# Differential attention: the weighted values from f16 high and low pieces, two banks for the transposes, the extreme kept scaled and negated

## The chip, the core and the metric

The kernel runs on one core of a Trainium2 chip. The metric is device time in microseconds of one execution; lower is better. TensorE (PE) multiplies and transposes, VectorE (DVE) and ScalarE (ACT) work on what it leaves in PSUM, GpSimd (POOL) takes a few element-wise steps, and SyncE (SP) issues most transfers. Each engine works through its own queue in order and waits on semaphores for the others.

## The reference, cut to what matters

One layer of a hybrid encoder: RMSNorm, one projection, four mixers (gated linear attention, a gated recurrence, differential attention, gated DeltaNet), a gated merge, cross attention over memory tokens, and a mixture of experts. The change touches differential attention alone. SEQ is 1024, there are 4 heads, two maps m of width 32 per head, and values 64 wide:

```python
        bias = -slopes[:, None, None] * dist
        s = jnp.einsum('bhmqd,bhmkd->bhmqk', q_blk, kt) + bias[None, :, None]
        p = jax.nn.softmax(s, axis=-1)
        attn = p[:, :, 0] - lam * p[:, :, 1]
        return jnp.einsum('bhqk,bhkd->bhqd', attn, vt)
```

After it each head's result is divided by its root mean square (`rmsnorm(o, norm_g)`), which takes any common factor out again, save for the small epsilon.

## The kernel before, in words

The dense products of the kernel are made in f16 pieces: a number is split into a high f16 and a low f16, and each product is three matmuls (high by high, high by low, low by high) at L709. Everything small is laid between these dense products by a list of steps that `plan_schedule` writes out: `dense(names, between=steps)` takes a step from the list, and for each `None` in it one portion of a dense product (six matmuls of 512 columns here). All engines walk the same list; each does its part of a step in that order.

Differential attention lies between the portions of the first merge (`merge(0)`, 80 portions). It has 32 units u, one for each head h and block qt of 128 queries. Of a unit:

- `diff_qk` (PE, L828): four f16 matmuls give the scores of both maps in PSUM banks 2 to 5. DVE (L2017) adds the distance row `DWH`, writes the sum to `DS[u % 2]` and keeps its maximum; L2022 multiplies the maximum by -1/sqrt(32).
- `diff_exp` (ACT, L1468): the exponential of both maps in place, with that number as bias; the row sums go to `d_l`.
- `diff_comb` (DVE, L2030 to L2036): a reciprocal, two tiny products, and one pass of 1024 elements that joins the two maps in `DS[u % 2][:, 0, :]`.
- `diff_tr` (PE, L841), twice per unit: four f32 transposes of 128x128 into bank 6. The first half is copied out by ACT (L1477), the second by DVE (L2044), into `DAT`, f32. Both halves use bank 6, so the second waits for ACT's copy of the first.
- `diff_pv` (PE, L851): eight f32 matmuls of 64 columns over `DAT` and the values `DVT`, into bank 7. The trace counts two instructions for each. ACT (L1484) scales the result into `DO`.

The unit loop is skewed: the scores of unit u+1 are made before the transposes of unit u. Between them lie the dense part's own steps. A gate product has four portions, and after the fourth ACT takes its tanh (L1249); the product after it ("up") has one portion, and DVE joins both (L1767). The next panel of weights is split in between by ACT (L1231, high piece) and DVE (L1744, low piece). Two units take five portions, and the pattern of these steps repeats after eight units. At the first unit of a head DVE also scales `DWH` (L2010). Before all this, the projections `dq`, `dk` and `dv` are copied out of PSUM; `emptied(g)` names the copy that PE waits for before it uses a bank again.

## Time and profile before

| | us |
|---|---|
| median of 3 runs | 2293.46 (2292.86 to 2296.08) |
| profiled execution | 2291.61 |
| its span | 2289.9 |
| PE busy in the span | 2038.0 (89%) |
| DVE busy | 1416.0 (62%) |
| ACT busy | 1079.6 (47%) |

The page's shares are means over stages with different limits. The differential attention stands from about 408 to 646 us, slices 8 to 12 of 40. A read of it needs the timeline: the same instruction is in the way in one unit and covered in the next. PE and PEld (loading of weights) overlap.

### The profile page before, as it was taken

Reading aid. Unit: us, or ns where it says so; the run is one execution under the profiler, and the core shown is the slowest. Engines: PE = TensorE matmul, PEld = TensorE weight load, DVE = VectorE, ACT = ScalarE, POOL = GpSimd, SP = SyncE. Lnnn points to the kernel's source line nnn. Section 1 sums busy time; section 2 is a strip of 40 time slices with the busy share of each in tenths; the row PEclk is TensorE's granted clock in tenths of the full one; section 3 lists DMA queues with packets and bytes.
Section 4 is the critical chain, followed back from the end, with each engine's and each line's share of the span. In section 5 each row is a group of like instructions: output and inputs, shape, how many; then the busy total and the mean of one; then the engine's idle time right before and its main releaser. Section 6 shows DMA issues by size and latency. Waiting matters only on the chain.

```text
span 2289.9 us, 31459 instructions
## 1 busy us (share of the span) xinstructions
PE 2038.0 (89%) x12278; PEld 1273.3 (56%) x12278; DVE 1416.0 (62%) x1864; ACT 1079.6 (47%) x1525; POOL 290.8 (13%) x335
## 2 busy tenths in 40 slices
PE   4999999899988787899899989999469999999991
PEld 3455465566644454788645875568435544444440
DVE  5455633688863475755433264543559999999976
ACT  4472223455545331110333353433248888888873
POOL 1010000000000563243021000000010111111102
PEclk9999999899999897999999999999779999999995
DMA  7111112111001134212311142040459999999986
GB/s 274 38 51 33 28 38 59 48 42 52 19 24 41 60 126 114 84 56 56 132 53 47 52 125 74 19 156 14 166 208 423 422 422 422 422 422 422 422 327 229
DMA packets 138212, 356.16 MB, mean 156 GB/s; under 512 B 37968, under 2 KB 91376, under 8 KB 111472
## 3 DMA queue, kind: packets, MB, share of 16 engines
q1 hardware_dynamic: 94304, 273.27, 31.4%
q10 hardware_dynamic: 34944, 48.24, 6.1%
q0 software_dynamic: 8848, 33.03, 3.7%
q8 instruction: 81, 1.33, 0.2%
q14 instruction: 35, 0.29, 0.0%
HBM read 305.74 MB, written 44.56 MB: 153 GB/s over the span
## 4 chain that ended last, share of the span: by engine, by line
PE 52%; DVE 7%; issue 2%; DMA 1%; ACT 1%; POOL 1%; ACTq 0%; POOLq 0%; DVEq 0%
PE psum L1084 22%; PE psum L709 20%; PE psum L960 1%; PE psum L1073 1%; DVE arena L2128 1%; DVE arena L2125 1%; PE psum L947 1%; PE psum L1012 1%; PE psum L1037 1%; PE psum L728 1%; PE psum L955 1%; PE psum L1102 1%; PE psum L1050 1%; PE psum L972 0%; POOL arena L2580 0%
## 5 line engine op out<-in xcount | busy, mean ns | idle before, releaser
L709 PE MATMUL psum<-arena 128*128 128x512 f16 (+2 forms) x6000 | 1021.0, 327 | 15.5 <-ACT arena L1249 10.1
L709 PEld LDWEIGHTS psum<-arena 128*128 128x128 f16 x6000 | 576.4, 99 | 390.1 <-issue 24.8
L1084 PE MATMUL psum<-arena 128*128 128x512 f16 x2304 | 514.6, 383 | 16.5 <-issue 9.5
L668 DVE SCALAR_TENSOR_TENSOR arena<-arena 128x2048 f16<-128x2048 f32 x192 | 437.8, 2287 | 78.9 <-ACT arena L663 78.7
L663 ACT ACTIVATE arena<-arena 128x2048 f16<-128x2048 f32 x192 | 365.5, 1908 | 66.0 <-DMA arena<-in_w_dram 36.8
L1084 PEld LDWEIGHTS psum<-arena 128*128 128x128 f16 x2304 | 225.2, 99 | 283.9 <-issue 22.6
L1744 DVE SCALAR_TENSOR_TENSOR arena<-arena 128x512 f16<-128x512 f32 (+1 forms) x212 | 140.7, 684 | 171.1 <-ACT arena L1231 171.0
L1231 ACT ACTIVATE arena<-arena 128x512 f16<-128x512 f32 (+1 forms) x212 | 126.4, 615 | 58.3 <-PE psum L709 11.1
L2441 POOL TENSOR_TENSOR arena<-arena 128x512 f32<-128x512 f32 x48 | 64.7, 1348 | 621.4 <-DVE arena L1767 621.4
L1249 ACT ACTIVATE arena<-psum,arena 128x512 f32<-128x512 f32 x64 | 43.7, 683 | 196.3 <-PE psum L709 188.5
L2565 POOL DMA_INDIRECT arena<-xhat,arena x32 | 63.6, 1988 | 508.1 <-PE psum L1073 447.0
L1767 DVE SCALAR_TENSOR_TENSOR arena<-arena,psum 128x512 f32<-128x512 f32 x64 | 43.8, 685 | 84.7 <-PE psum L709 65.6
L1310 ACT ACTIVATE arena<-psum 128x512 f32<-128x512 f32 (+3 forms) x51 | 29.8, 585 | 108.7 <-PE psum L709 108.7
L2017 DVE CUSTOM_DVE_ANT_0 arena<-psum,arena 128x1024 f32<-128x1024 f32 x64 | 77.9, 1217 | 3.4 <-PE psum L828 3.2
L1468 ACT ACTIVATE arena<-arena 128x1024 f32<-128x1024 f32 x64 | 73.3, 1146 | 10.7 <-DVE arena L2022 9.5
L1274 ACT ACTIVATE arena<-arena 128x256 f32<-128x256 f32 x64 | 26.6, 416 | 106.3 <-DVE arena L1773 105.3
L728 PE MATMUL psum<-arena 128*128 128x128 f32 x208 | 33.8, 319 | 43.6 <-DVE arena L1817 43.6
L851 PEld LDWEIGHTS psum<-arena 128*128 128x128 f32 x512 | 60.4, 192 | 15.3 <-issue 8.3
L851 PE MATMUL psum<-arena 128*128 128x64 f32 x512 | 62.3, 275 | 4.6 <-DVE arena L2044 3.6
L1773 DVE SCALAR_TENSOR_TENSOR arena<-psum,arena 128x512 f32<-128x512 f32 x32 | 22.1, 690 | 68.5 <-PE psum L709 68.5
L728 PEld LDWEIGHTS psum<-arena 128*128 128x128 f32 x208 | 29.1, 168 | 46.3 <-DVE arena L1817 45.6
L1788 DVE SCALAR_TENSOR_TENSOR arena<-psum,arena 128x512 f16<-128x512 f32 x32 | 22.1, 690 | 51.8 <-ACT arena L1263 27.6
(362 smaller groups left out, 2300.8 us busy)
## 6 DMA issues: line engine op xcount, KB each, us to landing
arena<-in_w_dram SPq DMA_DIRECT2D x192, 1024.0 KB, 11.9
arena<-in_merge_w_dram SPq DMA_DIRECT2D x64, 256.0 KB, 3.1
yrows<-arena ACTq DMA_DIRECT2D x32, 512.0 KB, 7.9
arena<-in_w_in_dram SPq DMA_DIRECT2D x48, 256.0 KB, 2.8
gdn_lq<-arena ACTq DMA_DIRECT2D x8, 1024.0 KB, 4.3
arena<-gdn_lq ACTq DMA_DIRECT2D x8, 1024.0 KB, 4.9
arena<-in_xattn_wkv_dram SPq DMA_DIRECT2D x32, 256.0 KB, 3.0
yrows<-arena POOLq DMA_DIRECT2D x1, 7680.0 KB, 31.4
```

The source lines that it names most:

```text
L663: nc.scalar.activation(half_of(XW[m][0], half), half_of(XLAND[m], half), ACT.Copy, scale=WS).then_inc(w_hi[m], 1)
L668: nc.vector.scalar_tensor_tensor(half_of(XW[m][1], half), half_of(XLAND[m], half), WS, half_of(XW[m][0], half), ALU.mult, ALU.subtract).th ...
L709: mm = nc.tensor.matmul(bank[prt[0]:prt[1], c0:c1], lhs[a](k), rhs[b](k), start=(k == 0 and a + b == 0), stop=(k == nk - 1 and a == 1))
L728: tr = nc.tensor.transpose(PS[:, 2 + 2 * (tt % 2) + k // 4, (k % 4) * P:(k % 4) * P + P], row_of(which, tt)[:, k * P:k * P + P], ident)
L851: mm = nc.tensor.matmul(PS[:, 7, 0:64], DAT[u % 2][:, k, :], DVT[:, k, h * 64:h * 64 + 64], start=k == 0, stop=k == TT - 1)
L1084: mm = nc.tensor.matmul(PS[:, bank, :], left[a][:, k, :], right[b][:, k, columns], start=k + a + b == 0, stop=(k == n - 1 and a == 1))
L1231: S.activation(W[i % 2][0][:, 2 * j:2 * j + 2, 0:wide], LAND[c % NLAND][:, :, 0:wide], ACT.Copy, scale=WS).then_inc(*act_hi.mark(c))
L1468: S.activation(DS[u % 2][:, m, :], DS[u % 2][:, m, :], ACT.Exp, scale=32 ** -0.5, bias=d_mx[u % 2][:, m:m + 1], accum_out=d_l[u % 2][:, m: ...
L1744: V.scalar_tensor_tensor(W[i % 2][1][:, 2 * j:2 * j + 2, 0:wide], LAND[c % NLAND][:, :, 0:wide], WS, W[i % 2][0][:, 2 * j:2 * j + 2, 0:wid ...
L2017: V.tensor_tensor_reduce(out=DS[u % 2][:, m, :], in0=PS[:, 2 + 2 * m:4 + 2 * m, :].rearrange("p a b -> p (a b)"), in1=DWH[:, 896 - P * qt: ...
L2441: G.tensor_tensor(dst, dst, SG[2 + (gate_no[n] - 1) % 2], ALU.add).then_inc(*counter("pool_merge").mark(n))
L2565: G.indirect_dma_start(XR[e % 2], None, XH_D, bass.IndirectOffsetOnAxis(IDX[:, e:e + 1], 0)).then_inc(rows_in[e % 2], 16)
```

## The change

The values are kept as f16 high and low pieces: ACT writes the high one as before, and DVE a low one (`dv` joins the branch that `dq` and `dk` take, so PE waits for DVE's copy of `dv`). The transposed weights are copied out in two pieces as well: ACT copies 16 times each half as f16, DVE the remainder as f16. The product is then three f16 matmuls for each of eight blocks. The factor 16 is taken out again in the final norm. The two halves of the transpose use banks 6 and 7 and are issued one behind the other; the product goes into bank 6. The two tiny products of `diff_comb` become one instruction. The maximum is kept as the minimum of the sum times -1/sqrt(32), so that it serves as bias at once.

```diff
-        diff += [("diff_qk", u + 1)] * more + [("diff_tr", u, 0), None] + [("diff_exp", u + 1)] * more
+        diff += [("diff_qk", u + 1)] * more + [("diff_tr", u, 0), ("diff_tr", u, 1), None] + [("diff_exp", u + 1)] * more
...
-        diff += [("diff_tr", u, 1), None] + [("diff_comb", u + 1)] * more + [("diff_pv", u)] + [None] * (u % 2)
+        diff += [None] + [("diff_comb", u + 1)] * more + [("diff_pv", u)] + [None] * (u % 2)
...
-        DVT = f32(BR + 4096, TT, 256)
+        DVT = (f16(BR + 4096, TT, 256), f16(BR + 5120, TT, 256))
...
-        DAT = [f32(BR + 16128 + 1024 * s, TT, P) for s in range(2)]
+        DAT = [(f16(BR + 16128 + 1024 * s, TT, P), f16(BR + 16640 + 1024 * s, TT, P)) for s in range(2)]
...
-            if kind[0] in ("up", "mix", "wo", "wk", "wv", "wq", "dq", "dk"):
+            if kind[0] in ("up", "mix", "wo", "wk", "wv", "wq", "dq", "dk", "dv"):
...
                     if u == 0:
-                        pe.wait_ge(*counter("act_evac").at(g_of["dv", 3]))
+                        pe.wait_ge(*counter("vec_evac").at(g_of["dv", 3]))
...
-                    if r:
-                        pe.wait_ge(*a.at("at", u, 0))
-                    else:
+                    if r == 0:
                         pe.wait_ge(*v.at("comb", u))
                         if u:
-                            pe.wait_ge(*v.at("at", u - 1, 1))
+                            pe.wait_ge(*a.at("o", u - 1))
+                    elif u:
+                        pe.wait_ge(*v.at("at", u - 1, 1))
                     for k in range(4):
-                        tr = nc.tensor.transpose(PS[:, 6, k * P:k * P + P], DS[u % 2][:, 0, (4 * r + k) * P:(4 * r + k + 1) * P], ident)
+                        tr = nc.tensor.transpose(PS[:, 6 + r, k * P:k * P + P], DS[u % 2][:, 0, (4 * r + k) * P:(4 * r + k + 1) * P], ident)
...
-                    if u:
-                        pe.wait_ge(*a.at("o", u - 1))
                     pe.wait_ge(*v.at("at", u, 1))
                     for k in range(TT):
-                        mm = nc.tensor.matmul(PS[:, 7, 0:64], DAT[u % 2][:, k, :], DVT[:, k, h * 64:h * 64 + 64],
-                                              start=k == 0, stop=k == TT - 1)
+                        for x, y in ((0, 0), (0, 1), (1, 0)):
+                            mm = nc.tensor.matmul(PS[:, 6, 0:64], DAT[u % 2][x][:, k, :], DVT[y][:, k, h * 64:h * 64 + 64],
+                                                  start=k + x + y == 0, stop=(k == TT - 1 and x == 1))
...
-                        act.wait_ge(*v.at("nm", u, m))
-                        S.activation(DS[u % 2][:, m, :], DS[u % 2][:, m, :], ACT.Exp, scale=32 ** -0.5,
+                        act.wait_ge(*v.at("max", u, m))
+                        S.activation(DS[u % 2][:, m, :], DS[u % 2][:, m, :], ACT.Exp, scale=-1.0,
...
-                    S.activation(DAT[u % 2][:, 0:4, :], PS[:, 6, :].rearrange("p (k n) -> p k n", k=4), ACT.Copy)\
-                        .then_inc(*a.mark("at", u, 0))
+                    S.activation(DAT[u % 2][0][:, 4 * r:4 * r + 4, :], PS[:, 6 + r, :].rearrange("p (k n) -> p k n", k=4), ACT.Copy,
+                                 scale=PSCALE).then_inc(*a.mark("at", u, r))
...
+                        elif name == "dv":
+                            hi, lo = (DVT[s][:, 2 * kind[1]:2 * kind[1] + 2, :] for s in range(2))
+                            src = bank.rearrange("p (a b) -> p a b", a=2)
...
-                                               in1=DWH[:, 896 - P * qt:896 - P * qt + T], scale=1.0, scalar=-3e38,
-                                               op0=ALU.add, op1=ALU.max, accum_out=d_mx[u % 2][:, m:m + 1])\
+                                               in1=DWH[:, 896 - P * qt:896 - P * qt + T], scale=-32 ** -0.5, scalar=3e38,
+                                               op0=ALU.add, op1=ALU.min, accum_out=d_mx[u % 2][:, m:m + 1])\
                             .then_inc(*v.mark("max", u, m))
-                        dve.wait_ge(*v.last())
-                        V.tensor_scalar(d_mx[u % 2][:, m:m + 1], d_mx[u % 2][:, m:m + 1], -32 ** -0.5, None, ALU.mult)\
-                            .then_inc(*v.mark("nm", u, m))
...
-                    V.tensor_tensor(d_c[u % 2], d_l[u % 2][:, 0:1], d_rl[u % 2][:, 1:2], ALU.mult).then_inc(*v.mark("c0", u))
-                    dve.wait_ge(*v.last())
-                    V.tensor_tensor(d_c[u % 2], d_c[u % 2], d_lam[:, 3:4], ALU.mult).then_inc(*v.mark("c", u))
+                    V.scalar_tensor_tensor(d_c[u % 2], d_l[u % 2][:, 0:1], d_rl[u % 2][:, 1:2], d_lam[:, 3:4], ALU.mult, ALU.mult)\
+                        .then_inc(*v.mark("c", u))
...
-                    dve.wait_ge(*q.at("tr", u, 1))
+                    dve.wait_ge(*a.at("at", u, r))
...
-                    V.tensor_copy(DAT[u % 2][:, 4:8, :], PS[:, 6, :].rearrange("p (k n) -> p k n", k=4)).then_inc(*v.mark("at", u, 1))
+                    V.scalar_tensor_tensor(DAT[u % 2][1][:, 4 * r:4 * r + 4, :], PS[:, 6 + r, :].rearrange("p (k n) -> p k n", k=4),
+                                           PSCALE, DAT[u % 2][0][:, 4 * r:4 * r + 4, :], ALU.mult, ALU.subtract).then_inc(*v.mark("at", u, r))
```

TensorE, from the scores of unit 5 to the product of unit 4. Before (L828 scores, L841 transposes, L709 dense, L851 product with the values; the count is of matmuls in the program), and the scores of unit 6 behind:

```order
L828 MATMUL psum<-arena 128x512 x4
L841 MATMUL psum<-arena 128x128 x4
L709 MATMUL psum<-arena 128x512 x6
L841 MATMUL psum<-arena 128x128 x4
L709 MATMUL psum<-arena 128x512 x6
L851 MATMUL psum<-arena 128x64 x8
L828 MATMUL psum<-arena 128x512 x4
```

The same place in the changed kernel (its lines stand one further up to L842):

```order
L829 MATMUL psum<-arena 128x512 x4
L842 MATMUL psum<-arena 128x128 x8
L710 MATMUL psum<-arena 128x512 x12
L851 MATMUL psum<-arena 128x64 x24
L829 MATMUL psum<-arena 128x512 x4
```

The two halves of the transpose now stand together, and both dense portions stand between them and the product, which has 24 matmuls in place of 8.

ScalarE in unit 5, before: the copy of the first half, the high piece of a weight tile, both exponentials of unit 6, the tanh of a gate, and the result of unit 5:

```order
L1477 ACTIVATE arena<-psum 128x512
L1231 ACTIVATE arena<-arena 128x512
L1468 ACTIVATE arena<-arena 128x1024 x2
L1249 ACTIVATE arena<-psum,arena 128x512
L1484 ACTIVATE arena<-psum,arena 128x64
```

The same in the changed kernel:

```order
L1478 ACTIVATE arena<-psum 128x512 x2
L1231 ACTIVATE arena<-arena 128x512
L1469 ACTIVATE arena<-arena 128x1024 x2
L1249 ACTIVATE arena<-psum,arena 128x512
L1485 ACTIVATE arena<-psum,arena 128x64
```

A second copy now stands ahead of the weight tile and of the exponentials.

VectorE in the same place, before (L2017 and its reading of the accumulator are the two rows ISA; then the copy of the second half, the low piece of the weight tile, and the joining of unit 6):

```order
L2017 ISA arena<-psum,arena 128x1024
L2017 ISA arena 128x1
L2022 TENSOR_SCALAR arena<-arena 128x1
L2017 ISA arena<-psum,arena 128x1024
L2017 ISA arena 128x1
L2022 TENSOR_SCALAR arena<-arena 128x1
L1744 SCALAR_TENSOR_TENSOR arena<-arena 128x512
L2044 COPY arena<-psum 128x512
L2030 RECIPROCAL arena<-arena 128x2
L2032 TENSOR_TENSOR arena<-arena 128x1
L2034 TENSOR_TENSOR arena<-arena 128x1
L2036 SCALAR_TENSOR_TENSOR arena<-arena 128x1024
```

The same in the changed kernel:

```order
L2021 ISA arena<-psum,arena 128x1024
L2021 ISA arena 128x1
L2021 ISA arena<-psum,arena 128x1024
L2021 ISA arena 128x1
L2044 SCALAR_TENSOR_TENSOR arena<-psum,arena 128x512 x2
L1745 SCALAR_TENSOR_TENSOR arena<-arena 128x512
L2031 RECIPROCAL arena<-arena 128x2
L2033 SCALAR_TENSOR_TENSOR arena<-arena 128x1
L2036 SCALAR_TENSOR_TENSOR arena<-arena 128x1024
```

Three of the tiny instructions are gone, and two passes (L2044) stand where one copy stood.

## Rows read from the trace of the kernel before

**Rows 1.** Page, part 2: the span in 40 slices, TensorE and its granted clock.

```profile
PE   4999999899988787899899989999469999999991
...
PEclk9999999899999897999999999999779999999995
```

**Rows 2.** Stretches: length, then busy time of each engine, clock, DMA share, GB/s.

```profile
455.00:480.00 25.00, 24.02 (x150) 15.47 (x148) 20.43 (x42) 13.10 (x25) 2.54 (x2) 1.00 0.28 74
480.00:505.00 25.00, 23.77 (x155) 16.23 (x154) 20.51 (x45) 14.77 (x27) 1.27 (x1) 1.00 0.07 22
416.00:420.00 4.00, 1.67 (x7) 1.00 (x6) 3.02 (x8) 0.89 (x3) 0.00 (x0) 0.50 0.08 27
```

**Rows 3.** Source line L2017: durations min/median/max in ns, first and last start.

```profile
L2017 DVE CUSTOM_DVE_ANT_0 arena<-psum,arena x64: 1212/1216/1225, 412.8 to 635.7; 128x1024 f32<-128x1024 f32 x64
```

**Rows 4.** Groups by form, 408 to 650 us: count, busy us, mean ns, idle before.

```profile
L851 PE MATMUL psum<-arena 128*128 128x64 f32 x512 | 62.3, 275 | 4.6 <-DVE arena L2044 3.6 <-ACT arena L1468 0.9
...
L2044 DVE COPY arena<-psum 128x512 f32<-128x512 f32 x32 | 22.1, 690 | 3.8 <-PE psum L841 3.8
```

**Rows 5.** Timeline 449 to 456 us: start, duration, engine, line, operation [idle before].

```profile
449.65 1.22 DVE L2017 CUSTOM_DVE_ANT_0 arena<-psum,arena 128x1024 f32<-128x1024 f32 x1
...
450.91 0.15 DVE L2022 TENSOR_SCALAR arena<-arena 128x1 f32<-128x1 f32 x1
450.98 1.22 DVE L2017 CUSTOM_DVE_ANT_0 arena<-psum,arena 128x1024 f32<-128x1024 f32 x1
...
451.16 1.15 ACT L1468 ACTIVATE arena<-arena 128x1024 f32<-128x1024 f32 x1 [0.34 <-DVE arena L2022]
...
452.43 1.15 ACT L1468 ACTIVATE arena<-arena 128x1024 f32<-128x1024 f32 x1
...
453.15 1.97 PE L851 MATMUL psum<-arena 128*128 128x64 f32 x16
...
453.70 0.17 DVE L2030 RECIPROCAL arena<-arena 128x2 f32<-128x2 f32 x1 [0.69 <-ACT arena L1468]
...
454.29 1.28 DVE L2036 SCALAR_TENSOR_TENSOR arena<-arena 128x1024 f32<-128x1024 f32 x1
...
454.96 1.03 PE L828 MATMUL psum<-arena 128*128 128x512 f16 x4
...
455.59 1.22 DVE L2017 CUSTOM_DVE_ANT_0 arena<-psum,arena 128x1024 f32<-128x1024 f32 x1
```

**Rows 6.** Timeline 438 to 443 us.

```profile
438.95 0.61 ACT L1231 ACTIVATE arena<-arena 128x512 f16<-128x512 f32 x1
439.60 0.69 DVE L1744 SCALAR_TENSOR_TENSOR arena<-arena 128x512 f16<-128x512 f32 x1 [1.21 <-ACT arena L1231]
...
440.79 1.28 DVE L2036 SCALAR_TENSOR_TENSOR arena<-arena 128x1024 f32<-128x1024 f32 x1
441.99 1.22 DVE L2017 CUSTOM_DVE_ANT_0 arena<-psum,arena 128x1024 f32<-128x1024 f32 x1
...
442.82 0.60 ACT L1477 ACTIVATE arena<-psum 128x512 f32<-128x512 f32 x1 [1.97 <-PE psum L841]
```

**Rows 7.** Timeline 456 to 464 us.

```profile
456.95 0.62 ACT L1231 ACTIVATE arena<-arena 128x512 f16<-128x512 f32 x1
...
457.48 1.14 ACT L1468 ACTIVATE arena<-arena 128x1024 f32<-128x1024 f32 x1
...
458.61 1.13 ACT L1468 ACTIVATE arena<-arena 128x1024 f32<-128x1024 f32 x1
...
461.50 1.46 PE L709 MATMUL psum<-arena 128*128 128x512 f16 x6
...
463.05 0.69 DVE L1767 SCALAR_TENSOR_TENSOR arena<-arena,psum 128x512 f32<-128x512 f32 x1 [1.30 <-PE psum L709]
```

**Rows 8.** Stretch of one us in the products 16 columns wide (L709, f16).

```profile
103.50:104.50 1.00, 1.00 (x47) 1.00 (x44) 0.00 (x0) 0.92 (x2) 0.53 (x1) 1.00 1.07 282
```

**Rows 9.** Groups by form, DVE, 300 to 420 us.

```profile
L1788 DVE SCALAR_TENSOR_TENSOR arena<-psum,arena 128x512 f16<-128x512 f32 x8 | 5.5, 691 | 24.0 <-ACT arena L1310 23.9
```

More of the change, by code:

```diff
@@ L33 @@
 NLAND = 4
+PSCALE = 16.0
 NE = 32
@@ L476, in build @@
         FIN = {
-            "gla": dict(o=GO, gate=GOGT, tmp=GTMP, row=R_GLAN, scale=1.0, y=1),
-            "diff": dict(o=DO, gate=None, tmp=DTMP, row=R_DIFFN, scale=0.8, y=0),
-            "gdn": dict(o=NO, gate=NZT, tmp=NTMP, row=R_GDNN, scale=1.0, y=1),
+            "gla": dict(o=GO, gate=GOGT, tmp=GTMP, row=R_GLAN, scale=1.0, times=1.0, y=1),
+            "diff": dict(o=DO, gate=None, tmp=DTMP, row=R_DIFFN, scale=0.8 / PSCALE, times=PSCALE, y=0),
+            "gdn": dict(o=NO, gate=NZT, tmp=NTMP, row=R_GDNN, scale=1.0, times=1.0, y=1),
         }
@@ L1277, in _ @@
                         if name in ("gv", "gog", "dv", "nz"):
-                            dst = {"gv": GVT, "gog": GOGT, "dv": DVT, "nz": NZT}[name][:, 2 * kind[1]:2 * kind[1] + 2, :]
+                            dst = {"gv": GVT, "gog": GOGT, "dv": DVT[0], "nz": NZT}[name][:, 2 * kind[1]:2 * kind[1] + 2, :]
                             src = bank.rearrange("p (a b) -> p a b", a=2)
@@ L1434, in _ @@
                     act.wait_ge(*v.at("ss", br))
-                    S.activation(fin_r, fin_ss, ACT.Ln, scale=1 / 64, bias=eps_col).then_inc(*a.mark("ln", br))
+                    S.activation(fin_r, fin_ss, ACT.Ln, scale=1 / 64 / f["times"] ** 2, bias=eps_col).then_inc(*a.mark("ln", br))
                     act.wait_ge(*a.last())
@@ L1483, in _ @@
                     act.wait_ge(*q.at("o", u))
-                    S.activation(DO[:, qt, h * 64:h * 64 + 64], PS[:, 7, 0:64], ACT.Copy, scale=d_rl[u % 2][:, 0:1])\
+                    S.activation(DO[:, qt, h * 64:h * 64 + 64], PS[:, 6, 0:64], ACT.Copy, scale=d_rl[u % 2][:, 0:1])\
                         .then_inc(*a.mark("o", u))
@@ L1774, in _ @@
                             .then_inc(*e.mark(n))
-                    elif name in ("wk", "wv", "wq", "dq", "dk"):
+                    elif name in ("wk", "wv", "wq", "dq", "dk", "dv"):
                         dve.wait_ge(*counter("act_evac").at(n))
@@ L2037, in _ @@
                         .then_inc(*v.mark("comb", u))
-                elif what == "diff_tr" and step[2] == 1:
-                    u = step[1]
-                    v, q = counter("vec_diff"), counter("pe_diff")
-                    dve.wait_ge(*q.at("tr", u, 1))
+                elif what == "diff_tr":
+                    u, r = step[1:]
+                    v, a, q = counter("vec_diff"), counter("act_diff"), counter("pe_diff")
+                    dve.wait_ge(*a.at("at", u, r))
                     if u >= 2:
                         dve.wait_ge(*q.at("o", u - 2))
-                    V.tensor_copy(DAT[u % 2][:, 4:8, :], PS[:, 6, :].rearrange("p (k n) -> p k n", k=4)).then_inc(*v.mark("at", u, 1))
+                    V.scalar_tensor_tensor(DAT[u % 2][1][:, 4 * r:4 * r + 4, :], PS[:, 6 + r, :].rearrange("p (k n) -> p k n", k=4),
+                                           PSCALE, DAT[u % 2][0][:, 4 * r:4 * r + 4, :], ALU.mult, ALU.subtract).then_inc(*v.mark("at", u, r))
                 elif what == "gdn_conv":
```

6 lines of the change are left out of this document (3 added, 3 removed).

## The prediction

> **What bounds the kernel now.** I read the page's slices first. In the stage of the change TensorE stands at 8 or 9 tenths at a granted clock of 9 tenths or more, so the mean says that PE bounds it [rows 1]. The stretches say the same more sharply: 24.02 and 23.77 of 25 us busy at clock 1.00, while DVE has 20.4 and 20.5 us and ACT 13 to 15 [rows 2]. DVE at 82% is close behind, so I went on to the timeline, to see what DVE waits for. The first addition of scores starts at 412.8 and the last at 635.7; less the 1.3 us between the two maps, that is 222 us over 31 units, 7.15 us each, or 57.2 for the eight units after which the pattern of dense steps repeats [rows 3].
>
> One round of the softmax is a loop through DVE and ACT. I count from the start of the first addition (449.65). Its scaled maximum is ready at 451.06, the first exponential starts at 451.16 (+1.51), the second at 452.43, the reciprocal at 453.70 (+4.05), the joining pass at 454.29, and the next addition at 455.59 [rows 5]. That is 5.94 us with nothing of the dense part on it. So of 7.15 us a round, 5.9 are this loop, and the rest is what the dense part lays into it or PE is late with. The stage is bound by two things at once, PE's queue and the loop; whatever PE is spared is given only up to the loop.
>
> **What PE is spared.** The product with the values takes 453.15 to 454.96, 1.81 us for 16 instructions [rows 5], 0.11 us each, and there are 512 of them [rows 4]. The 24 f16 matmuls of 64 columns have no row. From below: f16 matmuls of 16 columns with a load of weights each run at 47 in one us, 21 ns [rows 8]. From above: the f32 row's own 0.11 us. The six of 512 columns take 1.46 us until the last has ended [rows 7], under 0.24 us each, so the f16 load is not what they cost; by columns, 64 are 64/512 of that, 30 ns. I take 28 ns: 24 x 0.028 = 0.67 us, 1.1 us less a unit. Ends kept: 0.5 and 2.6 us a unit. Were PE alone the bound, 32 x 1.1 = 35 us would go.
>
> The f32 row shows 0.11 us for 64 columns, the f16 row 21 ns for 16 [rows 4, 8]. The Trainium skill speaks against the small matmul (TensorE: Matmul & The Clock Gate, "Back-to-back issue gap"): a stream of load-and-multiply pairs of 128 columns runs at about 81 ns each. By that rule 24 of them would be an estimated 1.94 us and the product would get dearer, not cheaper. The 21 ns of [rows 8] disagree with it as a floor, and the measurement decides.
>
> **What the loop gains and loses.** Terms, each from a row:
> - The scaled maximum goes. The addition ends at +1.22; with the 0.10 us that ACT took after L2022, the exponential can start at +1.32, the second at +2.55 (the second addition no longer has L2022 ahead of it, ends at about +2.45) [rows 5]. In the row above the exponentials stood 1.27 apart because the second waited for its maximum; where it did not wait they stood 1.13 apart (457.48, 458.61) [rows 7].
> - One of three tiny instructions of the joining goes: reciprocal to joining pass 0.59 before [rows 5], 0.40 after.
> - ACT gets a second copy ahead of the exponentials. After an addition that follows the joining at once, the copy of the first half starts at +0.83 (441.99 to 442.82) [rows 6]; ACT issues such passes 0.53 apart (456.95 to 457.48) [rows 7], taken as 0.5 to 0.53, so the exponential starts at +1.87 instead of +1.51. I call this a late round. Where a dense step stands on DVE between joining and addition (L1767, or the scaling of `DWH`), PE transposes under it and both copies are done by +1.3: an early round.
> - DVE gets two passes for one copy. A pass of this form took 691 ns [rows 9] against 690 for the copy [rows 4], and such passes stand 0.60 apart, less than their 0.69 (439.60, then 0.60 to what follows). They run from +2.45 to +3.65, and the reciprocal cannot start before +3.8: they fill the 0.69 us that DVE waited for ACT [rows 5]. This cover has 0.2 us left in an early round, 0.6 in a late one; if it is gone, what exceeds it is added in full.
>
> Second exponential to reciprocal 1.27, joining to the next addition 1.20 [rows 5, 6]. A late round is then 1.87 + 1.13 + 1.27 + 0.40 + 1.20 = 5.87, an early one 2.55 + 1.27 + 0.40 + 1.20 = 5.42, against 5.84 to 5.94 before.
>
> The dense steps: an L1231 between the copies and the exponentials adds 0.53 to ACT. One behind them is worse: it starts 1.15 after the second exponential, its L1744 0.65 later (438.95 to 439.60) [rows 6], and the reciprocal 0.60 behind that, 1.13 on the loop, before as after. An L1767 costs 0.60 between joining and addition, and waits for its product: 1.55 us from the portion's first matmul (461.50 to 463.05) [rows 7]. After unit 5 DVE idled 1.30 us for it [rows 7]; with the product 1.1 us shorter, and able to start when DVE's second piece is done (+3.75), the portion ends at about +5.95. So the eight rounds:
> - unit 0 (L1231 ahead; half early, as PE's queue ends with the addition): 6.2
> - 1 (late, L1231 behind, L1767): 5.87 + 1.13 + 0.60 = 7.6
> - 2 (early, L1231 behind): 6.55
> - 3 (late, L1744 and L1767 after the joining): 5.87 + 1.20 = 7.1
> - 4 (early, bare): 5.4
> - 5 (late, L1231 ahead, L1767): 5.87 + 0.53 + 0.60 = 7.0
> - 6 (early, scaling of `DWH` 1.2): 6.6
> - 7 (early, L1767 bound by the portion): 5.95 + 0.60 = 6.55
>
> Sum 53.0 against 57.2. For the units behind the first: three sets of eight save 3 x 4.2 = 12.6, five more (units 1 to 5, 33.7 against 5 x 7.15 = 35.7) save 2.0. In the first unit, where PE runs at clock 0.50 [rows 2], and behind the last, where nothing but PE's queue counts, each product saves its 1.1: 2.2. Together 16.8 us.
>
> PE's part in eight rounds is 0.96 x 57.2 - 8 x 1.1 = 46 us [rows 2], under 53; DVE's, 0.82 x 57.2 = 47 before, plus 8 x (0.60 - 2 x 0.08 - 0.20) = 2, is 49, under 53 too. The loop is what is late next.
>
> **Moved and added elsewhere.** The four low pieces of `dv`, 4 x 0.69 us on DVE, lie under dense products; the last stands about 0.7 us behind ACT's last copy. The scores of unit 0 wait for it, but their addition starts only at 412.8 [rows 3], behind ACT's distance row and its exponential of lambda, which don't hang on it. Cost 0; without this cover it is 0.7 once. PE's wait for ACT's result of the unit before (bank 6) moves from the product to the transposes; that result is out at about +5 (product done at +4.4, ACT free by then), the joining ends at +5.4 at the earliest: 0. If it came later than the joining, the next unit's transposes and both dense portions would queue behind it. No DMA is added or moved. What follows the stage starts earlier by the whole amount: fin's chain hangs on the last product just as before.
>
> The sum is against the profiled execution, 2291.61 us (span 2289.9, 1.7 around it): 2274.8. The median of the runs is 2293.46, 1.85 higher; against it, 2276.7, so 2277.
>
> **Rivals.**
> 1. PE's whole saving counts (35 us, 2259). For it: DVE and ACT are not full. Against: DVE's own part alone is 49 of 57.2, which allows 8.2 x 4 = 33 at most and only if every wait went.
> 2. The covers are too thin: the second copy makes all rounds late, and DVE's second pass stands out by 0.2. Then 0.45 more in half the units and 0.2 in all: 7 + 6 = 13 us back, 2290. For it: DVE has 0.2 us left in early rounds. Against: each spacing has a row.
> 3. Slower: the small f16 matmuls cost what the f32 ones do, 0.11 us. The place is the product's 24 instructions; 2.6 us for 1.81, +0.8 a unit. PE has 46 + 8 x (2.6 - 0.67) = 61.6 against 57.2: 4 x 4.4 = 18 us slower, 2311. It decides from (57.2 - 46 + 5.4) / 192 = 86 ns a matmul. The 81 ns of the rule above would lie just under it: by it, an estimate of no change. Against: 21 ns [rows 8].
> 4. The granted clock falls. PE idles about 1 us in each round now. At 0.50, as at 416 to 420 [rows 2], where PE had 1.67 of 4 us, its 5.8 us a round become 11.6. Each 4 us at half clock costs 2 us of PE, of which a round's slack takes 0.9; some 15 such stretches cost the gain, more make it slower. Against: the idle pieces lie under 1 us each, and slices at 8 tenths still show clocks of 8 and 9 tenths.
> 5. Nothing of it shows: the loop takes back all, 2293.
>
> **How the numbers follow.** Forecast 0.70 (own range 2271 to 2284); rival 1 0.03; rival 2 0.11; rival 3 0.04; rival 4 0.06; rival 5 0.06. Some 0.2% (4.6 us) is what a measurement of this kernel can tell from no change. Faster by more: the forecast, rival 1, and a good part of rival 2 and of 4: 0.83. Within: 0.10. Slower: rival 3 and a part of 4, 0.07. The range leaves out rivals 1, 3 and most of 5: 2268 to 2290.
>
> **What would show it.** Right: the product's 24 instructions in 0.6 to 0.8 us; additions (L2021) from first to last in about 207 us instead of 223; 5.4 us for the round of unit 4 of a set; DVE waiting before the reciprocal for ACT by 0.2 to 0.6 us; PE below 90% busy at clock 1.00. Wrong: PE still at 95% and above, the exponentials of early rounds behind +1.4, L2044 not done when ACT is, or a clock below 1.00 between 430 and 630 us.

## The result, and the profile after

The changed kernel has a median of 2276.36 us (2274.91 to 2278.07, 4 runs), the kernel before, run beside it on the same chip, 2294.77 (2292.86 to 2309.74, 4 runs). The ratio is 0.988, 95% interval 0.984 to 0.993: faster by 1.2%. The medians alone stand at 0.992. The execution at 2309.74 draws the ratio down; without it the means stand at 0.992 too. The time falls on the 2277 that was predicted; the gain against the kernel before is larger than the 0.7% that stood behind it. Two disturbed executions in the whole study, of 3608 and 7086 us, are left out of every number below.

The profiled execution took 2276.94 us (span 2275.2; before 2291.61, span 2289.9). What stands in the place of [rows 1], from the page of the changed kernel:

```profile
PE   4999999899988877899899999998479999999991
...
PEclk9999999999999988999999999999689999999995
```

The slices don't show it: TensorE still stands at 8 and 9 tenths in slices 8 to 12, though the stage is 19 us shorter. Its stretches (columns as in [rows 2]) do:

```profile
455.00:480.00 25.00, 23.34 (x204) 13.27 (x204) 23.02 (x41) 16.88 (x32) 2.55 (x2) 1.00 0.28 74
480.00:505.00 25.00, 21.88 (x177) 12.30 (x176) 22.30 (x38) 15.91 (x31) 2.54 (x2) 1.00 0.07 22
```

PE has gone from 24.0 and 23.8 of 25 us to 23.3 and 21.9; DVE from 20.4 to 23.0 and 22.3, as the same work and one pass more now fit into less time. The clock is 1.00 in both. The additions of scores, to be held against [rows 3], and the product's source line:

```profile
L2021 DVE CUSTOM_DVE_ANT_0 arena<-psum,arena x64: 1214/1218/1225, 415.5 to 620.3; 128x1024 f32<-128x1024 f32 x64
```

```profile
L851 PE MATMUL psum<-arena x768: 192/193/203, 427.1 to 628.9; 128*128 128x64 f16 x192
its engine sat idle before it (us, times) until:
  DVE arena L2044: 29.2, 45
```

First to last addition is 204.8 us, where it was 222.9. The 29.2 us of the last line are those of PE and of the loading of weights together. Taken by form, as in [rows 4], the matmuls of the product waited 4.6 us before and wait 8.4 now, all for DVE's passes; the transposes waited 5.1 us for the joining and wait 12.9:

```profile
L842 PE MATMUL psum<-arena 128*128 128x128 f32 x256 | 35.4, 282 | 12.9 <-DVE arena L2036 12.9
...
L851 PE MATMUL psum<-arena 128*128 128x64 f16 x768 | 27.8, 193 | 8.4 <-DVE arena L2044 8.4
```

So PE now waits for DVE on both sides of a unit. Here is the bare round, unit 4 of a set, in the timeline of the changed kernel; it answers to [rows 5]:

```profile
449.57 1.22 DVE L2021 CUSTOM_DVE_ANT_0 arena<-psum,arena 128x1024 f32<-128x1024 f32 x1
449.72 1.08 ACT L1478 ACTIVATE arena<-psum 128x512 f16<-128x512 f32 x2 [1.73 <-issue]
...
450.72 0.08 DVE L2021 DVE_READ_ACCUMULATOR2_ANT arena<- 128x1 f32 x1
450.72 1.22 DVE L2021 CUSTOM_DVE_ANT_0 arena<-psum,arena 128x1024 f32<-128x1024 f32 x1
450.90 1.15 ACT L1469 ACTIVATE arena<-arena 128x1024 f32<-128x1024 f32 x1
...
451.86 1.28 DVE L2044 SCALAR_TENSOR_TENSOR arena<-psum,arena 128x512 f16<-128x512 f32 x2
...
452.04 1.13 ACT L1469 ACTIVATE arena<-arena 128x1024 f32<-128x1024 f32 x1
...
453.20 0.87 PE L851 MATMUL psum<-arena 128*128 128x64 f16 x24 [0.54 <-DVE arena L2044]
453.30 0.17 DVE L2031 RECIPROCAL arena<-arena 128x2 f32<-128x2 f32 x1 [0.16 <-ACT arena L1469]
453.50 0.22 DVE L2033 SCALAR_TENSOR_TENSOR arena<-arena 128x1 f32<-128x1 f32 x1
453.75 1.28 DVE L2036 SCALAR_TENSOR_TENSOR arena<-arena 128x1024 f32<-128x1024 f32 x1
...
453.91 1.03 PE L829 MATMUL psum<-arena 128*128 128x512 f16 x4
...
454.96 1.22 DVE L2021 CUSTOM_DVE_ANT_0 arena<-psum,arena 128x1024 f32<-128x1024 f32 x1
```

The reader is to see three things. The next matmuls (L829) start 0.71 us behind the start of the 24, so each small one costs 29.6 ns. The first exponential starts 1.33 us after the addition, the second 1.14 behind it. And from addition to addition it is 5.39 us, with 0.16 us left between DVE's passes and the reciprocal.

Round by round (start of a first addition to the next), from the timelines of both kernels:

| | before | predicted | after |
|---|---|---|---|
| first unit of all, to the second | 5.85 | as before | 5.34 |
| behind it (PE at half clock at first) | 8.80 | -1.1 | 7.55 |
| a set of eight, three times | 57.25 | 53.0 | 52.80 |
| last five | 35.23 | -2.0 | 32.36 |
| last first addition to the dense matmuls behind the last product | 11.2 | -1.1 | 9.7 |
| stage | 232.9 | -16.8 | 213.4 |

So the stage gave 19.4 us. In these two executions 2.7 us of it stood against unchanged work ahead of the stage (the granted clock is lower in slices 2 to 4 of that execution, 0.94, 0.99 and 0.95 against 0.97, 1.00 and 1.00), and 2.0 behind it, which leaves the 14.7 between the two profiled times.

### The profile page after: what moved, and what is told of

Read it like the earlier page. It is cut to its first block, busy times and chain, and to the rows that moved or that the text cites. A ratio compares the mean times of both kernels' runs of the same rounds, so it can differ in the third digit from the quotient of the medians.

```text
span 2275.2 us, 31972 instructions
## 1 busy us (share of the span) xinstructions
PE 2011.8 (88%) x12534; PEld 1234.2 (54%) x12534; DVE 1423.9 (63%) x1804; ACT 1089.6 (48%) x1557; POOL 291.4 (13%) x335
## 4 chain that ended last, share of the span: by engine, by line
PE 53%; DVE 6%; issue 2%; DMA 1%; ACT 1%; POOL 1%; ACTq 0%; DVEq 0%; POOLq 0%
PE psum L1084 22%; PE psum L710 20%; PE psum L960 1%; PE psum L1073 1%; PE psum L1037 1%; PE psum L947 1%; PE psum L1012 1%; DVE arena L2129 1%; PE psum L729 1%; DVE arena L2126 1%; PE psum L1102 1%; PE psum L955 1%; PE psum L1050 1%; POOL arena L2581 0%; PE psum L972 0%
## 5 line engine op out<-in xcount | busy, mean ns | idle before, releaser
L1745 DVE SCALAR_TENSOR_TENSOR arena<-arena 128x512 f16<-128x512 f32 (+1 forms) x212 | 141.4, 686 | 154.0 <-ACT arena L1231 153.9
L1478 ACT ACTIVATE arena<-psum 128x512 f16<-128x512 f32 x64 | 34.8, 595 | 61.2 <-PE psum L842 37.5
L729 PEld LDWEIGHTS psum<-arena 128*128 128x128 f32 x208 | 28.7, 166 | 45.4 <-DVE arena L1821 44.8
L1660 ACT ACTIVATE arena<-psum 128x512 f16<-128x512 f32 x64 | 34.2, 584 | 33.4 <-PE psum L1073 33.4
```

What stands on the lines that cost most here:

```text
L729: tr = nc.tensor.transpose(PS[:, 2 + 2 * (tt % 2) + k // 4, (k % 4) * P:(k % 4) * P + P], row_of(which, tt)[:, k * P:k * P + P], ident)
L1745: V.scalar_tensor_tensor(W[i % 2][1][:, 2 * j:2 * j + 2, 0:wide], LAND[c % NLAND][:, :, 0:wide], WS, W[i % 2][0][:, 2 * j:2 * j + 2, 0:wid ...
```

## The experiments

All ratios are to the kernel before, run beside each on the same chip, with 95% intervals. "Stage length" is first to last addition in the trace: 222.9 before, 204.8 after.

**The changed kernel again**, in more rounds.

> The changed kernel once more, beside the kernel before on the same chip. The recorded pair gives two sizes for the gain: medians 2276.4 against 2294.8 (18 us, ratio 0.992), and a ratio of 0.9882 in which one run of before at 2309.7 weighs. The two profiles show the stage (first addition of scores to the end of the last product) 19.4 us shorter, 232.9 to 213.4, and the rest of the span within 5 us. If the stage is all, the ratio is 0.991 to 0.993 and the time 2274 to 2278. Rival: the ratio of 0.988 holds, 27 us, and something outside the stage gives 8 us: then this kernel stands below 2268 or before above 2300.

Measured: 2274.43 us (2268.29 to 2277.6, 6 runs), ratio 0.987 [0.983, 0.991], stage length 204.8. The gain is confirmed; its size is not. The time is where the stage alone would put it, but the kernel before stands at 2298.19 (29 runs), 23.8 us above, and the interval of the ratio reaches from 0.9 to 1.7%. Neither branch of what was expected came as a whole; the last experiments below say why.

**The small edits alone**: the kernel before with the extreme kept scaled and negated, and one tiny product.

```diff
-                        act.wait_ge(*v.at("nm", u, m))
-                        S.activation(..., scale=32 ** -0.5,
+                        act.wait_ge(*v.at("max", u, m))
+                        S.activation(..., scale=-1.0,
...
-                        V.tensor_scalar(d_mx[u % 2][:, m:m + 1], d_mx[u % 2][:, m:m + 1], -32 ** -0.5, None, ALU.mult)
```

> Kernel before with only the tiny edits: the extreme scaled and negated in the addition (L2022's multiplication gone), one tiny product for two. Loop theory (the round through addition, exponentials and joining bounds half of the units): the bare round falls from 5.9 to about 5.5, PE is then the bound in most rounds (about 55 of 57 us for eight), so 4 to 9 us come off, 2285 to 2290. PE theory (PE's queue alone bounds the stage): 0 to 1 us, 2293. First to last addition was 222.9 us: 214 to 219 by the loop, 222 by PE.

Measured: 2285.09 us (11 runs), ratio 0.993 [0.990, 0.996], stage length 213.4. Half of the stage's gain, 9.5 of 18.1 us, comes without any change to the product. A stretch of this kernel:

```profile
455.00:480.00 25.00, 24.88 (x156) 16.13 (x153) 20.02 (x35) 14.79 (x27) 2.55 (x2) 1.00 0.28 75
```

PE is busy 24.88 of 25 us: with the loop shorter, PE alone is the bound. The small edits together with the two banks, all else in f32, were not run; so how much of the other 8.6 us is the f16 product's own, and how much the place of the transposes gives beside it, is not shown.

**Two banks and adjacent transposes alone**, with f32 copies and the f32 product.

```diff
-... ("diff_tr", u, 0), None] ...
-... [("diff_tr", u, 1), None] + [("diff_comb", u + 1)] ...
+... ("diff_tr", u, 0), ("diff_tr", u, 1), None] ...
+... [None] + [("diff_comb", u + 1)] ...
-                        tr = nc.tensor.transpose(PS[:, 6, ...
+                        tr = nc.tensor.transpose(PS[:, 6 + r, ...
```

> Kernel before with only the two banks: both halves of the transposes together into banks 6 and 7, the product into bank 6, all in f32 as before, ACT copying the first half and DVE the second. Loop theory: nothing in the loop changes (the second copy on DVE stands behind the second addition anyway), 0 to 3 us off for PE's short waits, 2290 to 2294. Rival, the two banks are what brings the gain (the second transpose had to wait for ACT's copy): 10 us or more off, 2283 or less.

Measured: 2295.84 us (10 runs), ratio 0.998 [0.995, 1.001], stage length 219.5. The place of the transposes alone gives 3.4 us; that is too little for the interval to exclude no change.

**The changed kernel with the transposes in their old places.**

```diff
-... ("diff_tr", u, 0), ("diff_tr", u, 1), None] ...
-... [None] + [("diff_comb", u + 1)] ...
+... ("diff_tr", u, 0), None] ...
+... [("diff_tr", u, 1), None] + [("diff_comb", u + 1)] ...
```

> Changed kernel with the two halves of the transpose back in their old places (a dense portion and both exponentials of ScalarE between them); pieces in f16, two banks and tiny edits stay. PE's instructions are the same. Loop theory: ACT's second copy comes behind the second exponential, DVE's second piece behind that, and both before the reciprocal: 1.13 a round more, 31 rounds, minus what the late rounds win (0.45 in half of them): 25 to 35 us slower than the changed kernel, 2300 to 2310. PE theory: within 3 us of it, 2273 to 2280.

Measured: 2306.32 us (10 runs), ratio 1.002 [0.999, 1.005], stage length 235.3: all of the gain is lost and 12 us more in the stage, as expected. Its timeline shows where:

```profile
452.57 0.68 DVE L2044 SCALAR_TENSOR_TENSOR arena<-psum,arena 128x512 f16<-128x512 f32 x1
...
452.75 1.14 ACT L1469 ACTIVATE arena<-arena 128x1024 f32<-128x1024 f32 x1
...
453.88 0.58 ACT L1478 ACTIVATE arena<-psum 128x512 f16<-128x512 f32 x1
454.49 0.69 DVE L2044 SCALAR_TENSOR_TENSOR arena<-psum,arena 128x512 f16<-128x512 f32 x1 [1.24 <-ACT arena L1478]
...
455.23 0.87 PE L851 MATMUL psum<-arena 128*128 128x64 f16 x24 [1.44 <-DVE arena L2044]
```

ACT's second copy (L1478) stands in its queue behind both exponentials, DVE's pass waits 1.24 us for it, and the product 1.44 us for that. The f16 product needs every weight to pass both ACT and DVE; only with both transposes ahead of the exponentials does this lie beside them.

A small part of the loss is the clock. In the round of unit 7 of each set PE waits 2.33 us for DVE, and the stretch holds a granted clock of 0.50 for a while (0.75 on the mean of 5 us):

```profile
477.69 1.46 PE L851 MATMUL psum<-arena 128*128 128x64 f16 x24 [2.33 <-DVE arena L2044]
478.96 2.41 PE L710 MATMUL psum<-arena 128*128 128x512 f16 x6
...
481.21 1.03 PE L829 MATMUL psum<-arena 128*128 128x512 f16 x4
```

```profile
475.00:480.00 5.00, 2.67 (x29) 1.71 (x28) 2.97 (x7) 2.80 (x7) 0.00 (x0) 0.75 0.66 185
```

That round takes 9.35 us for 6.51; its product and the six dense matmuls behind it take 3.52 us (477.69 to 481.21), where it is 2.0 at full clock, some 4.5 us more in three sets (an estimate from these rows). In the changed kernel the clock is 1.00 from 430 to 630 us.

**The product made twice, and three times**; the last counts.

```diff
-                        for x, y in ((0, 0), (0, 1), (1, 0)):
+                        for r, (x, y) in enumerate(((0, 0), (0, 1), (1, 0)) * 2):
```

> Changed kernel with each of the 24 small matmuls of the product issued twice (48 a unit; the accumulated sum is twice as large, which the final norm takes out). It adds 24 x 0.029 = 0.69 us of PE a unit, 22 us in 32 units. PE theory (every PE microsecond counts): 22 us slower than the changed kernel, 2297. Loop theory: the first part goes into PE's idle time. By the walk of the rounds about 2.9 us of the 5.5 added in eight units come through (where the merge portion behind the product is waited for, and where the next scores come late): 10 to 15 us slower, 2286 to 2291; first to last addition 204.8 becomes 215 to 219.

> The changed kernel with the product with the values made three times (72 matmuls in place of 24), the last one counting. PE gets 1.35 us more in each of the 32 units, 43 us in all. The second product cost only 7.6 us of its 21.6 us, the rest went into time in which PE waited for DVE and ACT. Theory: this reserve is used up, the third product costs nearly its whole price, so the additions lie 228 to 234 us apart and the time is about 2300. Rival: the rounds keep reserve, and the third costs no more than the second: 220 us, about 2290.

Measured: 2282.69 us (6 runs), ratio 0.991 [0.988, 0.994], and 2297.71 us (12 runs), ratio 0.998 [0.995, 1.001]; stage lengths 212.4 and 227.6. PE's work grows each time by 32 x 0.67 to 0.71, some 22 us. The first portion costs 7.6 us in the stage, less than expected, the second 15.2, a little less than expected too. The same stretch of both:

```profile
455.00:480.00 25.00, 23.98 (x292) 15.57 (x293) 21.85 (x37) 14.26 (x29) 2.56 (x2) 1.00 0.28 76
```

```profile
455.00:480.00 25.00, 24.57 (x362) 16.48 (x360) 21.55 (x37) 15.01 (x29) 1.28 (x1) 1.00 0.20 49
480.00:505.00 25.00, 24.78 (x333) 16.42 (x330) 20.06 (x36) 13.84 (x27) 2.56 (x2) 1.00 0.15 49
```

The first is of the product made twice, the two others of three times. With 72 matmuls PE is nearly full (24.57 and 24.78 of 25), and of the last portion's 22 us two thirds come through; of the first portion's two thirds go into PE's waits. PE alone, the rival that would have given all of its 35 us, is refuted.

**The product of the high pieces only**, 8 matmuls for 24; it leaves out the low pieces in the product, not their making.

```diff
-                        for x, y in ((0, 0), (0, 1), (1, 0)):
-                            mm = nc.tensor.matmul(PS[:, 6, 0:64], DAT[u % 2][x][:, k, :], DVT[y][...
+                        mm = nc.tensor.matmul(PS[:, 6, 0:64], DAT[u % 2][0][:, k, :], DVT[0][...
```

> Changed kernel with the product of the high pieces alone: 8 matmuls a unit for 24 (the output is then that of f16 weights and values; all copies stay). It takes 16 x 0.029 = 0.46 us of PE from a unit, 15 us in all. PE theory: 15 us faster than the changed kernel. Loop theory: only the round in which DVE waits for the merge portion gains (0.4 in eight units), and the first and the last unit: 2 to 3 us faster, 2272 to 2274.

Measured: 2270.69 us (6 runs), ratio 0.987 [0.983, 0.990], stage length 204.1. Taking away another 0.45 us of PE's work a unit gives 0.7 us in the stage: PE is off the path. Round by round it gives what was expected, 0.47 in each of the three rounds of unit 7 and 0.35 in the second round of all. But 1.0 is lost again in one round, unit 3 of the second set, which takes 8.07 us for 7.06. There PE stood idle 1.74 us, and its work behind that took 1.97 and 3.49 us where it takes 1.04 and 2.75 at full clock:

```profile
492.21 1.97 PE L842 MATMUL psum<-arena 128*128 128x128 f32 x8 [1.74 <-DVE arena L2035]
493.98 3.49 PE L710 MATMUL psum<-arena 128*128 128x512 f16 x12
```

```profile
490.00:510.00 20.00, 17.18 (x104) 9.37 (x102) 17.77 (x31) 12.27 (x22) 1.27 (x1) 0.91 0.00 1
```

So the prediction's fourth rival, a granted clock that falls in this stage, shows one step further on: with PE spared still more it falls once between the additions and again behind the last one (0.72 from 620 to 624 us). Two other waits of 1.74 us in this trace were followed by no fall. It takes back a good part of what the smaller product gives. The median is 3.7 us under that of the changed kernel in another set of runs, which the stage doesn't bear out; I can't say whether it is more than spread.

**One copy of ACT's less.** DVE makes the second half as one f16 copy; its low piece is left out, and with it 4 matmuls a unit.

```diff
-                elif what == "diff_tr":
+                elif what == "diff_tr" and step[2] == 0:
...
+                    if r:
+                        V.tensor_scalar(DAT[u % 2][0][:, 4:8, :], PS[:, 7, :]..., PSCALE, None, ALU.mult)
```

> Changed kernel without ACT's second copy: the second half of the transposed weights goes out as one f16 copy by DVE (its low piece and the four matmuls over it are left out). DVE keeps two passes. Loop theory: in the late rounds (units 1, 3, 5 of eight, half of unit 0) the exponentials start 0.5 us earlier, the second still waits for its addition, so 0.45 a round: 1.5 in eight, 5 to 7 us faster than the changed kernel, 2268 to 2271. Rival (DVE's passes, not ACT's copy, end the round): 0 to 1 us. PE has 4 small matmuls less, 0.11 us a unit.

Measured: 2264.38 us (6 runs), ratio 0.984 [0.980, 0.987], stage length 196.1. 8.7 us, more than expected, come from one copy of 0.5 us a unit: the late rounds are late by it. Those of units 0, 1, 3 and 5 are 0.47 to 0.51 us shorter each, and the second round of all is 1.2 shorter. Before the reciprocal DVE waits 4.3 us in all instead of 10.5:

```profile
L2031 DVE RECIPROCAL arena<-arena x32: 156/166/167, 415.9 to 610.9; 128x2 f32<-128x2 f32 x32
its engine sat idle before it (us, times) until:
  ACT arena L1469: 4.3, 18
```

**The join ahead of the second dense portion.** In the rounds of units 1 and 2 DVE then no longer has the low piece of a weight tile (L1745) ahead of it, for which it waited 1.18 and 0.68 us.

```diff
-        diff += [None] + [("diff_comb", u + 1)] * more + [("diff_pv", u)] + [None] * (u % 2)
+        diff += [("diff_comb", u + 1)] * more + [None, ("diff_pv", u)] + [None] * (u % 2)
```

> Changed kernel with the joining of the two maps (diff_comb) one place earlier in the list, ahead of the second dense portion. PE's order stays. On DVE the low piece of a weight tile (L1745) then comes behind the joining instead of ahead of the reciprocal, in units 1 and 2 of each eight; there it waited about 1.1 us for ACT's high piece, which stands behind both exponentials. Loop theory: units 1 and 2 fall from 7.57 and 6.51 to about 7.1 and 6.0, 1.0 us in eight units, 4 us in all: 2270 to 2273. PE theory: nothing, 2274 to 2278.

Measured: 2271.54 us (6 runs), ratio 0.987 [0.983, 0.990], stage length 200.6, 4.2 less, as expected. A set of eight takes 51.54 us instead of 52.80.

**Why the ratio is larger than the stage.** 19.4 of 2293 us is 0.85%, the ratios say 1.2 and 1.3%. The executions of the kernel before fall into two groups: 40 of 65 took 2289.5 to 2302.7 us (median 2295.3), 25 took 2305.8 to 2317.0 (median 2313.3). The times alone leave only 3 us between the groups, but the mean granted clock parts them too: 0.951 and above in the short ones, 0.948 and below in the long ones. No profile of that kernel is of the second group, but those of two kernels next to it are. This is the router's stage, f32 transposes of 128x128 and f32 products of 36 columns, in the kernel with the small edits alone (span 2300.5, the longest of its 11 executions; the ten others took 2282 to 2288):

```profile
1590.00:1600.00 10.00, 4.69 (x43) 3.95 (x41) 1.31 (x4) 5.11 (x12) 0.72 (x6) 0.84 0.16 55
1600.00:1610.00 10.00, 8.92 (x43) 8.92 (x44) 7.20 (x7) 2.36 (x5) 0.00 (x0) 0.50 0.79 315
1610.00:1620.00 10.00, 10.00 (x50) 10.00 (x49) 2.75 (x4) 2.14 (x5) 0.00 (x0) 0.50 0.43 143
1620.00:1630.00 10.00, 10.00 (x50) 10.00 (x49) 0.00 (x0) 2.14 (x5) 0.00 (x0) 0.50 1.01 402
1630.00:1640.00 10.00, 10.00 (x49) 10.00 (x49) 0.00 (x0) 5.63 (x6) 0.00 (x0) 0.50 0.08 34
```

And in the profile of the changed kernel:

```profile
1590.00:1600.00 10.00, 6.66 (x45) 6.66 (x46) 7.54 (x7) 4.29 (x9) 0.00 (x0) 0.66 0.67 263
1600.00:1610.00 10.00, 10.00 (x94) 10.00 (x94) 2.66 (x4) 4.07 (x8) 0.00 (x0) 1.00 0.88 307
```

In both PE comes from 6.4 us without work, and the granted clock has fallen to 0.50 (1.2 GHz). In one it is back at 1.00 (2.4 GHz) after its first 4 us of work, in the other it stays at 0.50 for the whole stage though PE is busy 10 of 10 us: 50 instructions in 10 us instead of 94. From the first transposes to the last product of 36 columns it is 40.4 us in the one and 22.9 in the other. These 17.5 us are what the groups lie apart, 18.0:

```profile
1601.08 3.67 PE L728 MATMUL psum<-arena 128*128 128x128 f32 x16 [6.40 <-DVE arena L1817]
...
1634.63 6.88 PE L1050 MATMUL psum<-arena 128*128 128x36 f32 x32
```

```profile
1593.34 3.68 PE L729 MATMUL psum<-arena 128*128 128x128 f32 x16 [6.40 <-DVE arena L1821]
...
1612.59 3.66 PE L1050 MATMUL psum<-arena 128*128 128x36 f32 x32
```

To test that this is what parts the groups, 24 matmuls of 512 columns, results unused, were put on PE into those 6.4 us, in the kernel before, in the changed one, and in the one with the join moved:

```diff
+                    if which == "x2" and tt == 0:
+                        for _ in range(24):
+                            nc.tensor.matmul(PS[:, 7, :], XO[0][:, 0, 0:P], XO[0][:, 1, 0:512], start=True, stop=True)
```

> The kernel before with 24 extra f16 matmuls of 512 columns, results unused, put on PE into its 6.4 us of idle time ahead of the router stage. Theory: the router stage sometimes runs through at a granted clock of 0.50, because PE comes to it from an idle stretch and only brings transposes and 36-column products, and this makes such executions 15 to 18 us longer; before has them in 13 of 43 executions, the changed kernel in none of its own. With PE busy ahead of the stage no execution falls into it: all of them lie within 2286 to 2299, median about 2292, and in the trace the windows of the router stage show 1.00. Rival: the extra matmuls don't decide the clock, and some executions still lie at 2308 to 2316.

> The changed kernel with the same 24 extra matmuls. Theory: the stage of attention gives 18 to 19 us and nothing else does; against the kernel before with the same extra matmuls, on the same chip, this is 18 to 20 us faster: about 2273. Rival: a gap of 24 us or more stays between the two, and then something outside the stage gives 5 us or more.

> The changed kernel with the join of two heads issued ahead of the second dense portion, and the same 24 extra matmuls. Theory: the join's place gives the 3 to 4 us that it gave without them, so about 2269 to 2270, additions first to last 200 to 201 us. Rival: the gain seen without them was the spread of a few executions, and this lies within 1 us of the changed kernel with the extra matmuls.

Measured, on one chip:

| | us | executions | stage length |
|---|---|---|---|
| before, as it is | 2305.75 (2289.5 to 2317.0) | 23, of which 12 in the long group | |
| before, with the extra matmuls | 2293.81 (2290.1 to 2301.7) | 12, none long | 222.4 |
| changed, with them | 2273.97 (2273.3 to 2275.5) | 5 | 204.9 |
| join moved, with them | 2268.99 (2267.2 to 2270.0) | 6 | 200.5 |

With the extra matmuls the router's stage of the kernel before runs at full clock:

```profile
1610.00:1620.00 10.00, 8.61 (x53) 5.20 (x50) 5.86 (x7) 6.26 (x12) 0.70 (x6) 1.00 0.46 174
1620.00:1630.00 10.00, 10.00 (x94) 10.00 (x93) 5.01 (x6) 3.93 (x8) 0.00 (x0) 1.00 1.01 346
```

The long group is gone: none of 12, against 12 of 23 beside it. The change gives 19.8 us, a ratio of the medians of 0.991. The stage accounts for 18.9 of it in these two traces (232.4 to 213.4, counted as in the table of rounds); the last microsecond is within the spread. The ratios to the kernel before as it is are 0.996 [0.993, 0.999] for the same with the extra matmuls, 0.987 [0.982, 0.992] for the changed one and 0.985 [0.981, 0.989] for the last. The last is the fastest of these three; its 5.0 us over the changed one are the join's 4.4 and little more.

## Why the prediction was right, and where it was wrong

The time, 2277 for 2276.36, was right; the gain of 0.7% was not, since the measured interval (0.74 to 1.6%) lies above it. That the time came within 0.6 us is luck in part: the stage gave 2.6 us more than the sum, 4.7 us got lost ahead of it and behind it in the profiled execution, and the same kernel had medians of 2274.43 and, with the extra matmuls, 2273.97 in later sets. By its steps:

- **"28 ns: 24 x 0.028 = 0.67 us, 1.1 us less a unit."** Right: 0.71 us, 29.6 ns each. But the 21 ns from below were a misreading of [rows 8]: its 47 are all instructions that touch the microsecond, and as each lasts 169 ns, some seven of them began before it. From start to start it is 25 ns, (3.72 - 0.17) / 142:

```profile
102.44 3.72 PE L709 MATMUL psum<-arena 128*128 128x16 f16 x143
```

```profile
L709 PE MATMUL psum<-arena 128*128 128x16 f16 x143 | 3.7, 169 | 0.0
```

The Trainium skill's 81 ns for a pair of load and multiply (TensorE: Matmul & The Clock Gate, "Back-to-back issue gap") are for 128 columns. The prediction took them as a rule for 64, where the same section gives some 25 ns for 1 to 64 columns. The trace agrees with that at 16 columns, 25 ns; 64 columns took a little more.
- **"The stage is bound by two things at once ... whatever PE is spared is given only up to the loop."** Right, and shown from both sides: spared another 15 us of work, PE gives 0.7 us; given 22 us more, it takes 7.6. With the small edits alone the loop is shorter and PE stands at 24.88 of 25. None of the parts alone would have done it: the small edits give 9.5 and the two banks 3.4 of the 18.1 us by themselves, and the f16 pieces without the moved transposes cost 22 us against the small edits alone (235.3 to 213.4).
- **The loop's terms.** First exponential at +1.33 (said +1.32), second +2.47 (+2.55), reciprocal +3.73 (+3.82), joining 0.45 behind it (0.40), addition 1.21 behind that (1.20): 5.39 for 5.42. The rounds of a set were said to be 6.2, 7.6, 6.55, 7.1, 5.4, 7.0, 6.6, 6.55 and are 6.23, 7.57, 6.51, 7.05, 5.39, 6.97, 6.57, 6.51.
- **"They fill the 0.69 us that DVE waited for ACT"**: right, 0.16 us is left in an early round. The second copy on ACT is what the late rounds pay for; that is the 8.7 us of the kernel without it.
- **"Together 16.8 us."** Too small by 2.6, and this is a term mis-sized. The sets gave 13.35 for 12.6. The ends were treated as if only the product counted there: the very first round also loses the two scalings of the maximum (0.5 us, said 0), the last five rounds gave 2.9 for 2.0, the first at half clock and the tail 1.25 and 1.5 for 1.1 each.
- **"Moved and added elsewhere ... Cost 0."** Nothing speaks against it. The first addition starts at 412.2 to 416.3 us in the ten profiles with the low piece of `dv`, and at 412.8 to 416.8 in the four without it. And all that the transposes wait for is the joining (12.9 us), never ACT's result.
- **The fourth rival, the clock.** It did not come in the changed kernel, 1.00 from 430 to 630 us. (The stage's first units run at 0.50 before and after; "9 tenths or more" overlooks that slice 8 of [rows 1] shows 8.) It did come in two kernels next to it, the one with the transposes in their old places and the one with the high pieces only, behind waits of PE of 2.33 and 1.74 us. In the changed kernel no wait of PE from 430 to 630 us is longer than 1.28.
- **The signs.** All that were named for "right" came but for two at the edge: PE is busy 172 of 190 us between 430 and 620, 90.6%, for "below 90%", and DVE waits 0.16 us in an early round for "0.2 to 0.6".
- **"What follows the stage starts earlier by the whole amount."** Right for the stage's markers behind it; 2 us got lost further on in that one execution.
- **"The median of the runs is 2293.46" as the time that the gain is taken from, and 0.2% as what can be told from no change.** This is the step that failed, beside the 2.6 us of the sum. Three executions, all of the short group, stood for a kernel of which 25 in 65 take 18 us more; none of the 10 executions of the changed kernel do. That difference has no term in the prediction, which asked of the clock only whether it falls in the stage of the change. On a mean it is worth 25/65 x 18 = 6.9 us (an estimate), the larger part of what the ratio has over the forecast. With the router's clock held the medians lie 19.8 us apart, 3.3 more than the 16.5 that were forecast; without, 18.4 in one set of runs and 23.8 in another.

**Open.** Why the changed kernel never falls into the long group. Of the 56 executions of kernels with the f16 product and without the extra matmuls none was long (the one with the old order and the one with three products among them, which are as long as the kernel before), of the small edits alone 1 in 11, of the two banks alone 2 in 10. So it goes with the f16 pieces, some 950 us ahead of the router, and not with the length; 1 in 11 is too few to tell the small edits from none. The traces show the same 6.4 us of idle time and the same instructions there in all; no run here shows what links the two.

## What to carry to other kernels

Where an engine stands at 96% and the chain of dependent steps at 5.9 of 7.15 us a round, take both down together: here the loop alone gave 9.5 of 18.1 us and then left PE full, and sparing PE further gave next to nothing. Walking one round instruction by instruction, with the spacing of starts from the trace (0.60 us for passes of 0.69), predicted a set of rounds to 0.4% (53.0 for 52.80). Take the spacing from starts, too, and not from a count in a short stretch, which takes in what began before it (47 in one us at 25 ns each). When a value needs a second engine's pass before its use, look at what stands ahead of that pass in the queue: here the stage takes 235.3 us with the second copy behind the exponentials and 204.8 with both ahead. And look at the spread of the times of the kernel that you start from before you trust a median of three: here a stage of small matmuls behind 6.4 us of idle time ran at either clock.

## What the runs showed of the hardware

- f16 matmuls of 16 columns, each with its own load of weights, start 25 ns apart, and 24 of 64 columns take 29.6 ns each, at a granted clock of 1.00; eight f32 ones of the same size took 1.81 us [rows 5].
- The reading of the accumulator (0.08 us) does not delay the next pass: the second addition starts with it, 1.15 us after the first (449.57, 450.72), though each lasts 1.22.
- After 6.4 us of idle time f32 transposes and 36-column f32 products ran on at a granted clock of 0.50 for 40 us at 10 of 10 us busy in two of the profiled executions, and went back to 1.00 after about 3 to 4 us in the others. With 24 f16 matmuls of 512 columns in the idle time none of 12 executions was long, against 12 of 23 without, and they cost nothing that shows: 2293.81 with them, 2293.58 for the 11 short ones without.
- Between dense matmuls at a clock of 1.00, PE's waits of 2.33 and 1.74 us were followed by a stretch at 0.50 (the old order, three times; the high pieces only, once in the stage). In the changed kernel, with no wait above 1.28 us, the clock stayed at 1.00 from 430 to 630 us.
